# One group of transposes ahead of a score chunk, and its low part ahead of that chunk's maximum, once in every head of an attention kernel

## The reference, cut to what matters

```python
s = (jnp.einsum('bqhd,bkhd->bhqk', qn, k_nope)
     + jnp.einsum('bqhr,bkr->bhqk', qr, k_rope)).astype(jnp.float32) * scale
mask = key_chunk[None, :] <= q_chunk[:, None]
s = jnp.where(mask[None, None], s, NEG_INF)
p = jax.nn.softmax(s, axis=-1).astype(v.dtype)
return jnp.einsum('bhqk,bkhd->bqhd', p, v)
```

## Time and profile before

| | us |
|---|---|
| runs (3), median | 2603.19 |
| the profiled execution's own time | 2603.13 |
| its span in the profile | 2601.3 |
| TensorE busy, share of the span | 2551.6 (98%) |
| VectorE busy | 1880.5 (72%) |
| ScalarE busy | 1442.6 (55%) |
| attention stage | about 554 to 1556 |

### The profile page before, as it was taken

The page is one execution under the profiler, slowest core; times in us unless marked ns, Lnnn a source line. Parts: engine busy times, 40 slices in busy tenths (PEclk is TensorE's granted clock), DMA queues, the critical chain, the costliest instruction groups (busy, mean ns, idle before and its releaser), DMA issues. The chain is left out here.

```text
span 2601.3 us, 48010 instructions
## 1 busy us (share of the span) xinstructions
PE 2551.6 (98%) x17333; PEld 2401.8 (92%) x17333; DVE 1880.5 (72%) x3854; ACT 1442.6 (55%) x3530; POOL 429.7 (17%) x203
## 2 busy tenths in 40 slices
PE   8999999999999999999999999999999999999998
PEld 7999999989998999999999987888999999999787
DVE  6547651149898988898889886688887667666766
ACT  4433332248888888888888871125445445444211
POOL 0000000013354545444444400000000000000000
PEclk9999999999999999999999999999999999999999
DMA  7555454322233343333333316755544544553443
GB/s 224 187 168 181 139 165 120 97 57 47 52 90 82 84 82 94 83 80 75 86 76 79 75 45 201 224 173 194 204 179 159 202 153 135 183 188 132 145 144 112
DMA packets 246081, 337.85 MB, mean 130 GB/s; under 512 B 86354, under 2 KB 182498, under 8 KB 233506
## 3 DMA queue, kind: packets, MB, share of 16 engines
q1 hardware_dynamic: 228018, 326.40, 42.3%
q10 hardware_dynamic: 17840, 8.52, 1.1%
HBM read 225.34 MB, written 109.51 MB: 129 GB/s over the span
## 5 line engine op out<-in xcount | busy, mean ns | idle before, releaser
L1300 DVE TENSOR_TENSOR b_pt_lo<-b_transposed,b_pt_hi 128x384 fp32r<-128x384 f32 (+4 forms) x784 | 429.1, 564 | 52.4 <-ACT b_pt_hi L1190 49.0
L1285 DVE TENSOR_REDUCE ground<-b_ring 128x1 f32<-128x384 f32 (+7 forms) x784 | 409.3, 527 | 60.0 <-PE b_ring L45 44.0
L1190 ACT ACTIVATE b_pt_hi<-b_transposed 128x384 fp32r<-128x384 f32 (+4 forms) x784 | 382.4, 502 | 121.5 <-PE b_transposed L1225 109.8
L1177 ACT ACTIVATE ground<-b_ring,ground 128x384 f32<-128x384 f32 (+7 forms) x784 | 436.2, 561 | 19.6 <-DVE ground L1290 12.2
L1225 PE MATMUL b_transposed<-identity,ground 128*128 128x128 f32 (+2 forms) x2448 | 380.6, 273 | 9.7 <-DVE b_pt_lo L1300 7.5
L1225 PEld LDWEIGHTS b_transposed<-identity,ground 128*128 128x128 f32 (+2 forms) x2448 | 280.3, 135 | 57.8 <-issue 27.6
L43 PE MATMUL b_ring<-region 128*128 128x384 f32 (+7 forms) x784 | 300.6, 384 | 5.5 <-ACT ground L1177 4.2
L43 PE MATMUL p_banks<-p_x_hi,big 128*128 128x258 f32 x896 | 254.2, 284 | 9.3 <-DVE big L603 9.3
L45 PE MATMUL b_ring<-region 128*128 128x384 f32 (+7 forms) x784 | 257.9, 329 | 0.0
L44 PE MATMUL b_ring<-region 128*128 128x384 f32 (+7 forms) x784 | 257.5, 328 | 0.0
L45 PE MATMUL p_banks<-p_x_hi,big 128*128 128x258 f32 x896 | 254.2, 284 | 0.0
(11 more groups left out here) (214 smaller groups left out, 6282.6 us busy)
## 6 DMA issues: line engine op xcount, KB each, us to landing
ground<-x_a SPq DMA_DIRECT2D x22, 1032.0 KB, 5.6
ground<-w_conv SPq DMA_DIRECT2D x32, 512.0 KB, 3.8
c_tiles<-w_conv SPq DMA_DIRECT2D x32, 512.0 KB, 4.0
c_ln<-weight_sums SPq DMA_DIRECT2D x16, 1024.0 KB, 7.5
c_tiles<-weight_sums SPq DMA_DIRECT2D x16, 1024.0 KB, 7.1
weight_sums<-c_tiles SPq DMA_DIRECT2D x9, 1024.0 KB, 3.9
keys<-ground SPq DMA_DIRECT2D x64, 129.0 KB, 5.7
queries<-ground SPq DMA_DIRECT2D x64, 129.0 KB, 2.8
```

The source lines that it names most:

```text
L1177: nc.scalar.activation(p[0:rows, n % PSLOTS, 0:w], banks[0:rows, n % RING, 0:w], ACT.Exp, bias=nmax[0:rows, tile % 8:tile % 8 + 1], accum_ ...
L1190: nc.scalar.activation(turned(pt_hi, g, u, nb)[:, :, tile_columns(u, j)], tb[:, n % 2, 0:nb, 0:rows], ACT.Copy).then_inc(pt_hi_done, 1)
L1285: ins = nc.vector.tensor_reduce(top, bank[0:rows, 0:w], AX, ALU.max, negate=(chunks == 1))
L1300: nc.vector.tensor_tensor(lo, tb[:, n % 2, 0:nb, 0:rows], hi.bitcast(F32), ALU.subtract).then_inc(pt_split, 1)
```

## The change

Two neighbours are exchanged in `TENSOR_ORDER` and two in `VECTOR_ORDER`; `SCALAR_ORDER` stays, and so do all instructions, shapes and waits.

```diff
 TENSOR_ORDER = (
-    "...TSTSSPSTTP"
+    "...TSTSSPTSTP"
     "TSTPSTSTPTSTSPTTPT"
 )
 VECTOR_ORDER = (
-    "...LLMMLLMMMLLLMLALMLMMLLM"
+    "...LLMMLLMMLMLLMLALMLMMLLM"
     "LL"
 )
```

More of the change, by code:

```diff
@@ L847 @@
 TENSOR_ORDER = (
-    "STPSTSTPTSTSSPSTTSSPTTSSPTSTSTSPSTSTSPTSSTSTPSTSPSTSTPSSTSTPSTSTPSTSTPTSTSPTSTPSTTPSTSTPSSTTPSTSTSSPSTTP"
+    "STPSTSTPTSTSSPSTTSSPTTSSPTSTSTSPSTSTSPTSSTSTPSTSPSTSTPSSTSTPSTSTPSTSTPTSTSPTSTPSTTPSTSTPSSTTPSTSTSSPTSTP"
     "TSTPSTSTPTSTSPTTPT"
@@ L855 @@
 VECTOR_ORDER = (
-    "LLMAMLLMMLMLMMLLMMLMLMLMLMMLMAMLMLMLAMLMMLMLAMLMLMMMLLAMLMLMLMLMLLAMLLMMLLMLMLAMMLLMMLLMMMLLLMLALMLMMLLM"
+    "LLMAMLLMMLMLMMLLMMLMLMLMLMMLMAMLMLMLAMLMMLMLAMLMLMMMLLAMLMLMLMLMLLAMLLMMLLMLMLAMMLLMMLLMMLMLLMLALMLMMLLM"
     "LL"
```

## The result

The changed kernel takes 2609.72 us (median of 8 runs, 2608.12 to 2612.16), the kernel before in runs beside it 2603.45 us (8 runs, 2600.78 to 2608.11). The ratio is 1.0027 with a 95% interval of 1.0018 to 1.0036: **slower by about 7 us (4.7 to 9.4)**, where 6.7 were forecast and 2609.8 us. That is 0.27%, and the interval does not reach down to 1. The two medians by themselves are 6.3 us apart. The profiled execution has a span of 2610.0 us.

A forecast was written before the change was run, and what follows sets the result against it. TensorE sets the end of the attention stage, with little room on VectorE and ScalarE. Sixteen heads each losing 0.42 us add 6.7 us to the profiled 2603.13 us, giving 2609.8 us; range 2605 to 2613 us.

The forecast's parts named there:

- The wait removed: On TensorE, transposes no longer wait for a low part and start at 2.50 instead of 2.85, gaining 0.35 us.
- The maximum later: On VectorE, masking starts at 1.96, delayed 0.20 us by the later score chunk and 0.28 by the low part.
- E382: Exponential on ScalarE behind the maximum, forecast to start at 2.89 us instead of 2.41, its accumulator read ending at 3.57.
- What is late next: On TensorE, the next score chunk waits for the exponential's accumulator read and starts at 3.62, 0.42 us later per head.
- Behind S387: After that score chunk, ScalarE and VectorE run at most 0.06 us behind TensorE's own shift, which is not won back.
- ScalarE's slack: ScalarE's longest idle time in a head, 1.14 us, ends with TensorE's transposes, so the others follow TensorE and move with it.
- The sum: Over the attention stage, 16 heads times 0.42 us add 6.7 us, giving 2609.8 us.
- The high bound: Upper limit of the loss: another 0.1 us lost at the next products, 0.6 us a head, 9.3 us in all.
- Rival 1: The next score chunk does not wait, so each head wins 0.36 us, 5.8 in all: 2597.4 us; chance 0.04.
- Rival 2: Short TensorE waits later in the head take the 0.42 us delay back, total stays 2603 us; chance 0.09.
- Rival 3: Products waiting for sums taken out on VectorE are pushed too, 0.6 us or more a head: 2613 us; chance 0.04.
- the 0.53 that the text worked out: By the skill's rule of hidden weight loads, a score chunk between transposes takes 0.53 us, not 0.60; total unmoved.

The follow-up runs named there:

- Run 1: Only TensorE's exchange (transposes ahead of a score chunk), VectorE's order as in the kernel before: 2603.46 us, ratio 1.0011 to the kernel before.
- Run 3: Changed kernel with one low part in every head cut to 16 of its 256 columns: 2602.74 us, ratio 1.0008 to the kernel before.
- Run 4: Kernel before with one low part in every head cut to 16 columns, order unchanged: 2598.27 us, ratio 0.9996 to the uncut kernel before.
- Run 2: Only VectorE's exchange (low part ahead of the maximum), TensorE's order as in the kernel before: 2617.16 us, ratio 1.0059 to the kernel before.
- Run 5: Changed kernel with a product moved ahead of the waiting score chunk and the next transposes on TensorE: 2608.44 us, ratio 1.0024 to the kernel before.
- run 6: Kernel before with another order on TensorE alone, a score chunk and transposes moved ahead of a product: 2613.32 us, ratio 1.0039 to the kernel before.

## Why the prediction was right

- **The wait removed**: T374 gains 0.36 us a head, as said (2.85 to 2.49).
- **The maximum later**: masking at 1.97 for 1.96, E382 at 2.90 for 2.89. Runs 1 and 3 show both of its parts: the later chunk alone puts the masking at 1.69, L372 adds 0.28, of which a narrow L372 gives 0.25 back.
- **What is late next**: S387 at 3.64 for 3.62. Run 4 shows the cover directly: with T374's wait mostly gone and E382 untouched, S387 moves by 0.06.
- **Behind S387**: over all heads the mean shift of S387 is 0.435 us, that of P183 0.457. Here the text was only nearly right. A score chunk of 400 columns that starts behind a wait holds TensorE 0.65 us (1042.78 to 1043.43), against 0.63 without one (mean over the heads); that is the 0.02 that is added. The forecast of 0.42 was short by 0.04 a head, 0.6 us in all.
- **ScalarE's slack**: the 1.14 us that the text calls its longest idle time in the head is the longest behind the change; ahead of H372 it idles 1.30. What follows from it holds: from P183's like to the next head's P180's like TensorE takes 55.19 us at the least before and 55.17 after, and the 15 such stretches add up to 837.5 and 837.7 us. Nothing is taken back there and nothing is added.
- **The sum**: 16 x 0.457 = 7.3 us by the starts, 7.0 by the ratio with an interval of 4.7 to 9.4, and 6.7 in the forecast. That the median came within 0.1 us of the forecast is in part luck; the places of the single steps, each within 0.02 us, are not. The high bound of 9.3 us was added up unevenly: it puts the further 0.1 onto the 0.48 of E382, while the sum goes by the 0.42 of S387, with which it would be 8.3.
- **Rival 1** (the gain) falls with run 4: it was decided at the point named, the end of E382's read. The Trainium skill's advice in "Perfetto Trace Analysis", section "Identifying Performance Opportunities", to find the gap and make what it waits for start sooner, was followed by the change; T374 did start sooner, and the total rose.
- **Rival 2** and **Rival 3** fall with the stretches behind P183, which are the same before and after, and rival 3 also with P183's own shift, 0.46 and not 0.6 or more. Run 2 agrees, where 15.2 us of delay arrive as 15.3. Run 5 shows a product (P183) that waits for a unit's sums on VectorE, as rival 3 spoke of, but such waits take the first wait's place and add nothing.
- S386 holds TensorE 0.61 us between transposes (1039.98 to 1040.59) and not the 0.53 that the text worked out from the Trainium skill's weight-load rule ("TensorE: Matmul & The Clock Gate", section "What happens when you issue a matmul"). It changed nothing in the total, as said: the two transposes ahead hold the engine only 0.13, where two of the five before are 0.19, so P181 starts at the same place.

## What to carry to other kernels

Before a wait is removed, compute when the next step on the same engine could have started by its own releasers. If that is later than the removed wait would allow, the gain is only what lies between there and the place where the step started before, here 0.06 us out of 0.36. An exchange of two steps on an in-order engine delays one chain for the other: follow both to where they come back to the bound engine. And for a moved step list every wait in the code, also those for free buffers, for all who follow it: run 6 went wrong by one (H372 for P180) that the profile before shows no wait for; only another high part, once in each head, has a short wait of that kind there.

## What the runs showed that I had not expected

The largest single losses in the attention stage are none of these waits. At one place of head 4 ScalarE and VectorE stand still together, in the kernel before for 2.60 and 2.91 us, in the changed kernel for 2.18 and 2.48. The releaser is called remote by the trace in three of the four marks. The fourth, VectorE's in the changed kernel, names a score matmul, but the chunk that it reads was finished at 832.99, more than 2 us before. The kernel before:

```profile
833.48 0.60 ACT L1190 ACTIVATE b_pt_hi<-b_transposed 128x512 fp32r<-128x512 f32 x1 [2.60 <-remote]
833.53 0.57 DVE L1285 TENSOR_REDUCE ground<-b_ring 128x1 f32<-128x400 f32 x1 [2.91 <-remote]
```

The changed kernel:

```profile
835.07 1.08 ACT L1190 ACTIVATE b_pt_hi<-b_transposed 128x512 fp32r<-128x512 f32 x2 [2.18 <-remote]
```

TensorE then waits for them too. All six other runs have the pause at the same step, with TensorE marks of 1.10 to 1.71 us where these two have 2.37 and 1.94, and smaller ones in other heads.

At this place, in these two profiles and in none of the six others, the granted TensorE clock falls to its lower level (1.2 GHz, printed as 0.50) for some 3.4 us, after TensorE stood idle: in the kernel before at the end of the pause, in the changed one 1.1 us behind it. So it is not at its upper level through the whole attention stage. The kernel before, then the changed one:

```profile
core 0: us, PE busy (x) PEld busy (x) DVE busy (x) ACT busy (x) POOL busy (x), PEclk, DMA share, GB/s
834.45:837.80 3.35, 2.85 (x11) 2.49 (x12) 2.48 (x5) 2.13 (x8) 0.00 (x0) 0.50 1.05 255
...
837.60:841.00 3.40, 3.40 (x16) 3.30 (x15) 2.27 (x4) 1.65 (x6) 0.00 (x0) 0.50 1.09 201
```

The steps from the first transposes behind the pause to the second product after them (T215 to P105) take 4.91 and 5.08 us there, and 3.53 or 3.54 in the six other profiles: 1.4 to 1.5 us each, in both kernels alike, so it is no part of what the change costs.

From P183's like to the next head's P180's like a head takes 55.2 us where nothing pauses, in every profile but that of run 6, whose order differs there. With the pauses the 15 stretches add up to 832.1 us (run 4) at the least and 837.7 (the changed kernel) at the most. So the pauses and the clock make up to 5.6 us of difference between profiled executions. Single runs of one kernel differ by 4 to 12 us; whether these pauses make that too is not shown, since most of those runs left no trace. No experiment touched the pauses, and what causes them stays open.
